# A first layer whose input is normed behind its turn

## The reference

```python
h = x * rsqrt(mean(x * x, axis=-1) + 1e-6) * norm_g[0]   # (256, 1024), one root per token
proj = h @ e_w_in[0]                                      # even layer: 28 tiles of 128 columns
```

## Time and profile before

| what | us |
|---|---|
| median of 3 runs | 1422.24 |
| the runs | 1418.95, 1422.24, 1422.52 |
| the profiled execution | 1418.69 |
| its span, first to last instruction | 1416.8 |

### The profile page before, as it was taken

The page is one execution under the profiler, slowest core; times in us unless marked ns, Lnnn a source line. Parts: engine busy times, 40 slices in busy tenths (PEclk is TensorE's granted clock), DMA queues, the critical chain, the costliest instruction groups (busy, mean ns, idle before and its releaser), DMA issues.

```text
span 1416.8 us, 28209 instructions
## 1 busy us (share of the span) xinstructions
PE 1364.0 (96%) x10866; PEld 1186.1 (84%) x10866; DVE 987.5 (70%) x1543; ACT 779.2 (55%) x1296; POOL 9.4 (1%) x23
## 2 busy tenths in 40 slices
PE   7998999999999999998999999999999999999997
PEld 7986887778888889877888888888889987888886
DVE  6977628977766677667766667766677856876665
ACT  6456547766555566334655455555555633655454
POOL 0000000000000000000000000000000000000000
PEclk9999999999999999999999999999999999999999
DMA  8732453246555555203565554555545401465551
GB/s 297 294 123 74 164 215 128 74 149 208 196 195 187 182 175 165 75 4 119 196 206 178 195 196 165 201 197 188 179 160 191 140 17 48 165 221 178 194 195 56
DMA packets 62789, 229.82 MB, mean 162 GB/s; under 512 B 7008, under 2 KB 7264, under 8 KB 62448
## 3 DMA queue, kind: packets, MB, share of 16 engines
q1 hardware_dynamic: 60912, 220.23, 45.9%
q0 software_dynamic: 1792, 8.37, 1.7%
HBM read 227.53 MB, written 1.05 MB: 161 GB/s over the span
## 4 chain that ended last, share of the span: by engine, by line
PE 87%; DVE 7%; ACT 4%; issue 2%; DMA 0%; DVEq 0%; SPq 0%; ACTq 0%
PE PS L793 23%; PE PS L1114 22%; PE PS L1135 17%; PE PS L1117 12%; PE PS L782 1%; PE PS L772 1%; PE PS L1321 1%; PE PS L1327 1%; DVE x_res L1961 1%; DVE w_lo L2035 1%; ACT arena L1578 1%; DVE out_operands L2057 1%; DVE arena L2086 1%; PE PS L1289 1%; PE PS L1336 1%
## 5 line engine op out<-in xcount | busy, mean ns | idle before, releaser
L1114 PE MATMUL PS<-hT_both,w_hi 128*128 128x512 f32 x1376 | 342.7, 391 | 0.0
L1114 PEld LDWEIGHTS PS<-hT_both,w_hi 128*128 128x128 f32 x1376 | 252.5, 188 | 48.6
L793 PE MATMUL PS<-hT_both,w_hi 128*128 128x256 f32 x1392 | 254.8, 285 | 2.0 <-DVE w_lo L2035 0.9
L793 PEld LDWEIGHTS PS<-hT_both,w_hi 128*128 128x128 f32 x1392 | 217.1, 192 | 6.1 <-issue 4.7
L2317 DVE TENSOR_TENSOR w_lo<-weight_ring,w_hi 128x1024 fp32r<-128x1024 f32 x176 | 207.1, 1218 | 2.4 <-ACT w_hi L1738 2.4
L1117 PEld LDWEIGHTS PS<-hT_both,w_lo 128*128 128x128 f32 x1376 | 187.7, 190 | 13.4
L793 PE MATMUL PS<-hT_both,w_lo 128*128 128x256 f32 x696 | 196.8, 283 | 0.0
L1117 PE MATMUL PS<-hT_both,w_lo 128*128 128x256 f32 x1376 | 191.8, 282 | 0.0
L2323 DVE TENSOR_TENSOR w_lo<-weight_ring,w_hi 128x1024 fp32r<-128x1024 f32 x88 | 107.8, 1225 | 104.0 <-ACT w_hi L1747 104.0
L1738 ACT ACTIVATE w_hi<-weight_ring 128x1024 fp32r<-128x1024 f32 x176 | 175.2, 1043 | 0.0
L2035 DVE TENSOR_TENSOR w_lo<-weight_ring,w_hi 128x1024 fp32r<-128x1024 f32 x107 | 126.0, 1221 | 47.9 <-ACT w_hi L1516 47.8
(11 more groups left out here) (309 smaller groups left out, 1823.3 us busy)
## 6 DMA issues: line engine op xcount, KB each, us to landing
weight_ring<-in_stream SPq DMA_DIRECT2D x411, 512.0 KB, 4.4
norm_gain<-in_gains_in POOLq DMA_DIRECT2D x8, 512.0 KB, 4.1
consts<-in_csts POOLq DMA_DIRECT2D x1, 1864.0 KB, 9.7
arena<-in_taps_in SPq DMA_DIRECT2D x4, 384.0 KB, 3.4
arena<-in_bias_in POOLq DMA_DIRECT2D x1, 1152.0 KB, 12.7
x_res<-in_x_in SPq DMA_DIRECT2D x2, 512.0 KB, 3.9
lora<-in_lora_in POOLq DMA_DIRECT2D x2, 512.0 KB, 3.7
x_out<-yT SPq DMA_DIRECT2D x2, 512.0 KB, 2.7
```

The lines of the kernel that those rows point to most:

```text
L793: ins = pe.matmul(out, w[a], x[b], start=(start and i == 0), stop=(stop and i == 2))
L1114: pe.matmul(PS[:, b, :], Wh[:, u, k, :], HT2[:, k], start=(k == 0), stop=(k == KT - 1), skip_group_check=True)
```

## The change

The first phase no longer norms x ahead of the turn. TensorE multiplies x, as it was loaded, by the diagonal matrix of its roots, which turns and scales in one matmul. The gain now lies along partitions, so it is a column per block of 128: VectorE multiplies the PSUM result by it (`first_gain`, 128x8, broadcast along the tokens), and ScalarE and VectorE split that.

- Loads: x's halves have a semaphore each; `ident` is issued between them; the 512 KB gain row is gone and a 4 KB gain column comes behind the second half.
- ScalarE: `late_root` for both token halves, then `first_split`: Hh parts 0 and 1, the split of weight tile 0, Hh parts 2 and 3, all read from SBUF and no longer from PSUM.
- VectorE: `first_seam`: two diagonals, gain on parts 0 and 1, Hl 0 and 1, gain on parts 2 and 3, W_lo of tile 0, Hl 2 and 3.
- TensorE: `high_first` waits for the tile's high part and, only ahead of its second pass, for its low part, in the three phases with projections.
- Four semaphores become two (`conv_stage`, `odd_exp_made`), with counts moved to match, and the counts of `xn_made`, `x_made`, `rstd_made` and `roots_spread` are moved.

```diff
@@ loads
             for t in range(NTT):
-                sp.dma_start(X[:, t, :], x_in[t * P:(t + 1) * P, :]).then_inc(sem("x_loaded"), 16)
-            sp.dma_start(G[:], gains_in[0:1, :].broadcast_to([P, D])).then_inc(sem("head_loaded"), 16)
-            sp.dma_start(CSTt[:, 0:CST_FIRST], csts[:, 0:CST_FIRST]).then_inc(sem("head_loaded"), 16)
+                sp.dma_start(X[:, t, :], x_in[t * P:(t + 1) * P, :]).then_inc(sem(f"x_loaded{t}"), 16)
+                if t == 0:
+                    sp.dma_start(CSTt[:, 0:CST_FIRST], csts[:, 0:CST_FIRST]).then_inc(sem("head_loaded"), 16)
+            sp.dma_start(first_gain[:], first_gain_in).then_inc(sem("head_loaded"), 16)
...
@@ TensorE
             def transposes_in(n):
                 for t in range(NTT):
+                    if n == 0:
+                        pe.wait_ge(sem("roots_spread"), t + 1)
                     for half in range(2):
...
+                            if n == 0:
+                                ins = pe.matmul(PS[:, turned_bank(n) + 2 * t + half, k * P:(k + 1) * P],
+                                                X[:, t, kk * P:(kk + 1) * P], root_diag[:, t, :], start=True, stop=True)
+                                continue
...
-            def high_first(n, u, near, far):
+            def high_first(n, u, near, far, tiles=None):
+                if tiles is not None:
+                    pe.wait_ge(sem("tile_hi"), tiles + 1)
                 for i, w in enumerate((Wh, Wl)):
+                    if tiles is not None and i == 1:
+                        pe.wait_ge(sem("tile_lo"), tiles + 1)
...
-                        is_split(i + 1)
                         u = (q + i) % RING
                         o = PS[:, b, i * T:(i + 1) * T]
                         if n == 0 and i == 0:
-                            ins = high_first(phase, u, o, o)
+                            ins = high_first(phase, u, o, o, tiles_before(phase))
                             continue
+                        is_split(i + 1)
...
@@ ScalarE
+            def first_split():
+                for i in range(4):
+                    if i == 2:
+                        ahead(0)
+                    act.wait_ge(sem("hT_scaled"), i + 1)
+                    half, cols = slice(4 * (i % 2), 4 * (i % 2) + 4), slice((i // 2) * P, (i // 2 + 1) * P)
+                    act.activation(Hh[:, half, cols], scaled_part(i), ACT.Copy).then_inc(sem("hT_hi"), 1)
...
+                elif n == 0:
+                    act.preload_act_table_set("natural_log_exp_and_others")
+                    for t in range(NTT):
+                        late_root(n, t)
+                    first_split()
...
@@ VectorE
             def roots_spread(n):
                 for t in range(NTT):
+                    if n == 0 and t == 0:
+                        dve.wait_ge(sem("head_loaded"), HEAD)
                     dve.wait_ge(sem("rstd_made"), roots_at(n) + t + 1)
-                    dve.tensor_scalar(half_root[:, t:t + 1], stat[:, 4 + t:5 + t], 0.5, None, ALU.mult)
+                    if n:
+                        dve.tensor_scalar(half_root[:, t:t + 1], stat[:, 4 + t:5 + t], 0.5, None, ALU.mult)
...
+            def first_seam():
+                roots_spread(0)
+                def split_part(i):
+                    half, cols = slice(4 * (i % 2), 4 * (i % 2) + 4), slice((i // 2) * P, (i // 2 + 1) * P)
+                    dve.wait_ge(sem("hT_hi"), i + 1)
+                    dve.tensor_tensor(Hl[:, half, cols], scaled_part(i), Hh[:, half, cols], ALU.subtract)\
+                       .then_inc(sem("hT_lo"), 1)
+                for i in range(4):
+                    dve.wait_ge(sem("xT_made"), i + 1)
+                    dve.tensor_tensor(scaled_part(i), PS[:, turned_bank(0) + i, :].rearrange("p (k t) -> p k t", k=4),
+                                      bc(first_gain[:, 4 * (i % 2):4 * (i % 2) + 4], P), ALU.mult)\
+                       .then_inc(sem("hT_scaled"), 1)
+                    if i == 1:
+                        split_part(0)
+                        split_part(1)
+                ahead(0)
+                split_part(2)
+                split_part(3)
```

More of the change, by code:

```diff
@@ L381, with build @@
 PAIR0 = {"even": 0, "odd": 4}
-def build(nc, x_in, stream, params, csts, bias_in, lora_in, gains_in, taps_in, vb2, sinks, out):
+def build(nc, x_in, stream, params, csts, bias_in, lora_in, gains_in, first_gain_in, taps_in, vb2, sinks, out):
     ctx = ExitStack()
@@ L634, in x_made_at, with roots_spread_at @@
         def x_made_at(n):
-            return sum((4 if m else 0) + (0 if late(m) else 2) for m in range(n + 1))
+            return sum((4 if m else 0) + (0 if late(m) or m == 0 else 2) for m in range(n + 1))
         def roots_at(n):
-            return sum(2 if late(m) else 4 for m in range(n))
+            return sum(2 if late(m) or m == 0 else 4 for m in range(n))
         def late_before(n):
             return sum(late(m) for m in range(n))
+        def roots_spread_at(n):
+            return NTT * (late_before(n) + 2)
         def turned_bank(n):
@@ L724, in gain @@
             def gain(n):
-                pool.wait_ge(sem("xn_made"), 4 * n)
+                if n > 1:
+                    pool.wait_ge(sem("xn_made"), 4 * (n - 1))
                 pool.dma_start(G[:], gains_in[n:n + 1, :].broadcast_to([P, D])).then_inc(sem("gain_loaded"), 16)
@@ L1474, in rstd @@
                     for half in range(2):
[L1475 to L1478, removed]
+                        act.wait_ge(sem("x_made"), x_made_at(n - 1) + 3 * t + half + 1)
                         ins = act.activation(squares[:, half * 512:(half + 1) * 512],
@@ L1484, in rstd @@
                     done.wait(done(ins))
-                    act.wait_ge(sem("x_made"), x_made_at(n - 1) + 3 * t + 3 if n else t + 1)
+                    act.wait_ge(sem("x_made"), x_made_at(n - 1) + 3 * t + 3)
                     done.wait(done(act.activation(stat[:, 6 + t:7 + t], stat[:, 2 * t + 1:2 * t + 2], ACT.Ln,
@@ L1491, in late_root @@
             def late_root(n, t):
-                act.wait_ge(sem("x_made"), x_made_at(n - 1) + 2 * t + 2)
+                if n:
+                    act.wait_ge(sem("x_made"), x_made_at(n - 1) + 2 * t + 2)
+                else:
+                    act.wait_ge(sem(f"x_loaded{t}"), 16)
                 done.wait(done(act.activation(squares, X[:, t, :], ACT.Square, accum_out=stat[:, t:t + 1])))
@@ L1926, in _ @@
                     late_root(n, 1)
+                elif n == 0:
+                    act.preload_act_table_set("natural_log_exp_and_others")
+                    for t in range(NTT):
+                        late_root(n, t)
+                    first_split()
                 else:
                     rstd(n)
-                    if n == 0:
-                        ahead(0)
                     hT_split(n)
@@ L1986, in normed @@
             def normed(n, t):
-                if n:
-                    dve.wait_ge(sem("gain_loaded"), 16 * n)
-                else:
-                    dve.wait_ge(sem("head_loaded"), HEAD)
+                dve.wait_ge(sem("gain_loaded"), 16 * n)
                 dve.wait_ge(sem("rstd_made"), roots_at(n) + 2 * t + 2)
@@ L1997, in inputs_normed @@
             def inputs_normed(n):
-                early = n > 0 and not PHASES[n - 1][0].startswith("ffn")
+                early = not PHASES[n - 1][0].startswith("ffn")
                 for t in range(NTT):
-                    if n:
-                        added_to_x(n - 1, t)
+                    added_to_x(n - 1, t)
                     biased(n, t)
@@ L2016, in seam @@
                     inputs_normed(n)
-                if n == 0:
-                    ahead(n)
                 for i in range(4):
```

37 lines of the change are left out of this document (22 added, 15 removed).

## The result

| | kernel before | kernel after |
|---|---|---|
| median, 13 runs each | 1421.75 us | 1427.95 us |
| lowest and highest | 1415.98, 1425.28 | 1422.67, 1430.16 |
| ratio after to before | | 1.005, 95% interval 1.0037 to 1.0064 |
| the profiled execution | 1418.69 us | 1428.22 us |

The change makes the kernel slower by half a per cent, some 6 to 7 us, where 0.7 us had been forecast with a range that ended at 1425.6. Later, 12 more runs of the kernel after, beside 31 of the kernel before, gave means 6.0 us apart again. One kernel's runs spread over 9 us.

What follows compares the result with a forecast made beforehand. TensorE, busy 96% of 1416.8 us, was taken as the bound, so weight tile 1's start decides. Its +0.74 us on 1418.69 gave 1419.4 in the profile's frame; 1420.6 + 0.7 gave the forecast, 1421.3 us, range 1417.8 to 1425.6.

Steps and rivals of the forecast that it cites:

- So whatever the change does to the start of weight tile 1 is carried through to the end, one for one: Head: TensorE is busy without a break from 16.03 to 60 us, so a shift of that start reaches the end whole.
- +0.74 us: Head: weight tile 1 starts on TensorE at 16.77 us against 16.03, the forecast's sum for the change.
- Edits at nothing: Merged semaphores, moved counts, split order, POOL's dropped gain load and two dropped bias instructions: they cost and save nothing.
- I take 6.0: Loads in the head: the 4 KB gain column lands at 6.0 us, between bounds of 5.6 and 8.54.
- rival B: Small load in the head: the gain column lands at 8.54 us, delaying the first diagonal; +3.3 us, 1423.9, chance 0.10.
- The reasoning that the gain row's bytes had made the identity late: Loads in the head: the identity's 6.4 us held the gain row's 512 KB, now gone, so the column lands earlier.
- it is a sixteenth of x's 1 MB, so it is worth 0.1 to 0.3 us: Loads in the head: the 64 KB identity between x's halves delays the second half slightly, to 5.6 us.
- Two instructions a matmul: First phase's turn on TensorE: float32 matmuls that are not transposes run as two instructions each, so 32 in all.
- If that repeats from 6.45, the rate rises at 9.5: First phase's turn: after 3.1 us of work, TensorE's instruction spacing falls from 0.215 to 0.11 us.
- Rival A: Clock in the head: rate rises only about 12.5 us, +1.4 us, or falls back before the first pass, +2.6; chance 0.18.
- The moved wait: TensorE's first pass: starts at 13.44 us before W_lo of tile 0 (14.38); otherwise 14.4, with tile 1 near 17.3.
- near 1418.8 and near 1422.4: Whole kernel: four earlier executions read as two levels, mean 1420.6 us; a median may fall on either.

Runs made afterwards that it cites:

- e3: The kernel before with the identity's load issued behind weight tile 1; 2.9 us slower than the kernel before, ratio 1.0002 to 1.0041.
- e13: The kernel before with 31 instructions of fulfilled waits on TensorE ahead of the second phase's turn; 6.3 us slower, ratio 1.0030 to 1.0066.
- e5: The kernel after with loads reordered (x's halves, identity, gain column) and the column awaited only before the first gain multiply; 3.5 us slower than the kernel before.
- e2: The kernel before with 31 instructions of fulfilled waits at TensorE's start; 2.7 us slower, ratio 0.9995 to 1.0039.
- e12: e5 with x multiplied by its roots on VectorE, sixteen transposes, and the gain applied in 128x128 copies and splits; 2.6 us slower than the kernel before.
- e7: The kernel before with 96 instructions of fulfilled waits at TensorE's start; 3.5 us slower, ratio 1.0003 to 1.0033.
- e10: The kernel after with 65 instructions of fulfilled waits at TensorE's start; 6.0 us slower than the kernel before, ratio 1.0023 to 1.0059.

## Why the prediction was wrong

**Where it looked: the step that failed.** "So whatever the change does to the start of weight tile 1 is carried through to the end, one for one" held as a sentence (e3: 2.5 us later in the trace, 2.9 in the time) and failed as a frame: the sum had the head for its only term, and +0.74 us for it. Measured were 6.0 us, of which the head is 2.2 (two profiles). "Edits at nothing" put the rest at nothing without a reason, and it has two terms. The doubled matmuls were counted and priced at 0.215 us where they stand, and not for the 31 places by which they move TensorE's later code. That is worth about 2 us in the mixers, and e13, with that move alone, is 6.3 us slower at its own low clock and some 2 to 4 at an equal one. The output projections' slower matmuls are the other, 1.0 us. With up to 1.1 us of clock this makes up the 6.0.

**The loads.** "I take 6.0" for the column and 5.6 for x's second half: they were 8.2 and 7.2. In size this is rival B, given 0.10, with +3.3 us; the head gave 3.1 in the profile (2.2 over the two profiles of the kernel after). In mechanism it is not: the small column was not slow by itself, for in e5 its 32 B pieces landed 3.8 us after issue. The reasoning that the gain row's bytes had made the identity late fits e5, where the column lands at 5.9. What failed is the step "it is a sixteenth of x's 1 MB, so it is worth 0.1 to 0.3 us": with the identity between the halves the second one landed 1.7 us later, half a microsecond of it by its later issue. I priced the small pieces for themselves and not for what stood behind them.

**The turn.** Two instructions a matmul: right (x32). "If that repeats from 6.45, the rate rises at 9.5": wrong. In the kernel after the turn ran from 8.62 to 12.8 at 421 ns, in e5 from 6.25 to 12.2. Rival A had priced this at +1.4 us over the kernel before, tile 1 at 17.65 in the chain's row; e5 has 17.25.

**VectorE and ScalarE.** 0.69 us for the gain multiply, 0.63 for the copies from SBUF, and VectorE without a gap from the second part on: all as worked out. The moved wait did what was said: the first pass began at 15.92, while tile 0's low part was ready only at 16.85.

**The clock.** Four executions had been taken as two levels "near 1418.8 and near 1422.4". Over 107 runs there are no two levels but a spread that follows the mean granted clock. (By the prediction's own terms, too, the range should have been 1418.1 to 1425.7.) Whether moved code lowers the clock is not shown: the seven kernels with it lie between 0.0032 below and 0.0008 above the kernel before beside them. The half-rate stretch in the kernel after's mixer begins 1.1 us behind the end of a wait on "issue" of 1.29 us, with TensorE busy in between; one execution cannot tell cause from chance. What made e2's rest (1.3) so much smaller than e13's (6.1) stays open, apart from errors of 1.2 us on either.

## What to carry to other kernels

Count what an edit adds to the instruction stream of the engine that sets the end, not only its time: in a program of unrolled short matmuls, each added instruction moves the code behind it, and 31 places were worth about 3 us of 1420 in the mean of seven kernels, 1.3 to 6.1 in the single ones. Look at what a new tile does to the addresses of the old ones, too. Test a change of under a per cent with a control that moves the code alike and does nothing. Don't put a load of many small pieces ahead of one that the first compute step waits for.

## What was not expected of the hardware

- TensorE waits for nothing visible for up to 1.8 us at places 256 records apart, where its matmuls are short; in the phases with long matmuls such places don't show.
- The 128x512 matmuls of the output projections last longer (393 ns for 389 in the kernel after) in all nine kernels with 32 B more per partition ahead of their operands.
- 64 KB in 512 B pieces made the 512 KB behind them land 1.7 us later, while behind x they landed 0.3 us after it (e5), and behind the gain row 1.1 us.
- VectorE multiplies 128x1024 float32 from SBUF by a column in 0.75 us (e12), less than twice what it takes for 128x512 with a second tensor (0.69).
- An instruction of two fulfilled waits costs TensorE 0.11 us in a row at the start of its code: with 96 of them the turn begins at 12.88 (e7), with 65 at 9.42 (e10).
